# A two-block transformer on one Trainium2 core: how half B of the residual is renewed in the turns of the second block

## The reference, cut to what matters

```
x = x + gt1 * rms_norm(y_lat, g_mix_post[i])
m_lat = sq_relu_mlp(modulate(rms_norm(x, g_mlp_pre[i]), sh2, sc2), w_mlp_in[i], w_mlp_out[i])
x = x + gt2 * rms_norm(m_lat, g_mlp_post[i])
# next layer: modulate(rms_norm(x, g_mix_pre[i + 1]), sh1, sc1), then the projection by w_qkv
```

## Time and profile before

| what | value |
|---|---|
| median of 3 runs | 3484.14 us (3482.54 to 3484.38) |
| the profiled execution, time | 3486.8 us |
| its span in the profile | 3485.0 us |
| PE busy | 3435.7 us (99%), 18494 instructions |
| DVE busy | 2166.1 us (62%), 3570 instructions |
| ACT busy | 1318.3 us (38%), 1951 instructions |
| POOL busy | 297.0 us (9%) |
| mean granted TensorE clock | 0.996 |

### The profile page before, as it was taken

The page is one execution under the profiler, slowest core; times in us unless marked ns, Lnnn a source line. Parts: engine busy times, 40 slices in busy tenths (PEclk is TensorE's granted clock), DMA queues, the critical chain, the costliest instruction groups (busy, mean ns, idle before and its releaser), DMA issues.

```text
span 3485.0 us, 46915 instructions
## 1 busy us (share of the span) xinstructions
PE 3435.7 (99%) x18494; PEld 2869.0 (82%) x18494; DVE 2166.1 (62%) x3570; ACT 1318.3 (38%) x1951; POOL 297.0 (9%) x376
## 2 busy tenths in 40 slices
PE   9999999999999999999999999999999999999998
PEld 7888967898888988895789888899988898588888
DVE  7555565656555655566676777788776557655444
ACT  4222453333222422246333523355523236643222
POOL 0000232001000100023100000012100001210000
PEclk9999999999999999999999999999999999999999
DMA  7544302434444344330243444345444311013221
GB/s 277 187 157 160 109 24 100 157 133 169 155 160 150 137 165 156 146 108 10 102 163 138 148 160 157 145 147 180 173 171 163 112 70 67 25 50 119 89 95 49
DMA packets 85562, 452.01 MB, mean 130 GB/s; under 512 B 10305, under 2 KB 12545, under 8 KB 48609
## 3 DMA queue, kind: packets, MB, share of 16 engines
q1 hardware_dynamic: 83168, 439.10, 34.2%
q0 software_dynamic: 2176, 9.92, 0.8%
HBM read 446.88 MB, written 2.10 MB: 129 GB/s over the span
## 4 chain that ended last, share of the span: by engine, by line
PE 89%; DVE 5%; ACT 3%; issue 1%; DMA 0%; POOL 0%; DVEq 0%; SPq 0%; ACTq 0%; POOLq 0%
PE ps L660 22%; PE ps L658 22%; PE ps L659 22%; PE ps L2774 2%; PE ps L2775 2%; PE ps L2776 2%; PE ps L3473 1%; PE ps L1035 1%; PE ps L1037 1%; ACT P L1855 1%; PE ps L1036 1%; PE ps L1772 1%; PE ps L1295 1%; PE ps L1297 1%; PE ps L1296 1%
## 5 line engine op out<-in xcount | busy, mean ns | idle before, releaser
L660 PE MATMUL ps<-nH,WL 128*128 128x512 f32 x2256 | 884.9, 392 | 0.0
L658 PE MATMUL ps<-nH,WH 128*128 128x512 f32 x2256 | 884.3, 392 | 0.4 <-ACT rot L3203 0.4
L659 PE MATMUL ps<-nL,WH 128*128 128x512 f32 x2256 | 883.1, 391 | 0.0
L564 DVE TENSOR_TENSOR WL<-raw,WH 128x2048 fp32r<-128x2048 f32 (+2 forms) x297 | 651.0, 2196 | 372.3 <-ACT WH L553 371.2
L553 ACT ACTIVATE WH<-raw 128x2048 fp32r<-128x2048 f32 (+2 forms) x299 | 543.3, 1822 | 574.4 <-PE ps L660 496.9
L658 PEld LDWEIGHTS ps<-nH,WH 128*128 128x128 f32 x2256 | 423.8, 188 | 95.2 <-issue 3.3
L659 PEld LDWEIGHTS ps<-nL,WH 128*128 128x128 f32 x2256 | 423.8, 188 | 93.7 <-issue 0.2
L660 PEld LDWEIGHTS ps<-nH,WL 128*128 128x128 f32 x2256 | 423.8, 188 | 91.5
L624 DVE SCALAR_TENSOR_TENSOR araw<-araw,cB 128x1024 f32<-128x1024 f32 x224 | 275.4, 1229 | 208.2 <-DMA araw<-in_ast 207.9
L658 PE MATMUL ps<-hH,WH 128*128 128x512 f32 x944 | 372.2, 394 | 1.0 <-DVE h L1262 1.0
L660 PE MATMUL ps<-hH,WL 128*128 128x512 f32 x944 | 371.3, 393 | 0.0
(11 more groups left out here) (452 smaller groups left out, 5919.6 us busy)
## 6 DMA issues: line engine op xcount, KB each, us to landing
raw<-in_wst SPq DMA_DIRECT2D x273, 1024.0 KB, 4.8
araw<-in_ast SPq DMA_DIRECT2D x225, 512.0 KB, 5.7
raw<-in_wst SPq DMA_DIRECT2D x18, 512.0 KB, 3.3
araw<-in_wst SPq DMA_DIRECT2D x9, 1024.0 KB, 4.8
row<-in_ast SPq DMA_DIRECT2D x15, 512.0 KB, 10.5
cw<-in_cw POOLq DMA_DIRECT2D x4, 1024.0 KB, 6.0
h<-in_xT SPq DMA_DIRECT2D x4, 512.0 KB, 5.5
raw<-in_wst SPq DMA_DIRECT2D x8, 256.0 KB, 2.7
```

The source lines that it names most:

```text
L564: dve.q.tensor_tensor(M.WL[k % NW][:, 0:n], M.raw[raw_use[k]][:, 0:n], M.WH[k % NW][:, 0:n].bitcast(F32), ALU.subtract).then_inc(*v_wlo.up(k))
L658: pe.q.matmul(to, hi[:, i, cc], xh, start=i == 0, stop=False)
L659: pe.q.matmul(to, hi[:, i, cc], xl, start=False, stop=False)
L660: t = pe.q.matmul(to, lo[:, i, cc], xh, start=False, stop=i == nk - 1)
```

## The change

It touches the first and the second turn. The third does what it did before.

1. ACT: half B's tiles of `ma` are multiplied by gain and gate on ACT (`gained(o)`), right behind square o for o = 0 to 5 and ahead of the split of weights in the same step; products 6 and 7 stand behind the root of half B. These are 8 more ACTIVATEs in each of the two turns.
2. DVE: half B is renewed two tiles at a time (`renew_pair`): 4 products and 4 additions of 128x2x256 instead of 8 and 8 of 128x256.
3. DVE: in step i, half A's `times` and `low` come ahead of the renewal.
4. DVE: the first half of the last split comes ahead of the pair of i = 4; the second half comes right behind the pair of i = 6, ahead of the additions of squares 5, 6 and 7, where it stood behind them.
5. ACT's squares of half B's renewed tiles wait for the pair (`i | 1`), and so do later readers of `h` (`was`).

```
             def renewed(x, i):
-                half_square_act(act, g + "AB"[x], lat.half[x], i, hs[x], lambda i: v_h.to(post + "AB"[x], i))
+                half_square_act(act, g + "AB"[x], lat.half[x], i, hs[x], lambda i: v_h.to(post + "AB"[x], i | x))
+
+            def gained(o):
+
+                act.wait_ge(*v_gain.to(post))
+                act.wait_ge(*a_sq.to(post + "B", o))
+                act.q.activation(ma[1](o), ma[1](o), ACT.Copy, scale=der(post)[:, o:o + 1]).then_inc(*a_gt.up(post, o))
...
-                else:
-                    act.wait_ge(*v_gain.to(post))
-                    act.wait_ge(*a_sq.to(post + "B", o))
-                    act.q.activation(ma[1](o), ma[1](o), ACT.Copy, scale=der(post)[:, o:o + 1]).then_inc(*a_gt.up(post, o))
+                if g is None or o < 6:
+                    gained(o)
                 split_act(act, k0 + (6 if o >= 4 else 5 if o == 3 else 4))
...
             half_root_act(act, post + "B", B)
+            gained(6)
+            gained(7)
             for i in range(8):
...
+            def renew_pair(i):
+
+                n = post + "B"
+                u, h = M.ma[:, i:i + 2, B.cols], M.h[:, i:i + 2, B.cols]
+                dve.wait_ge(*mm.to(n, "rstd"))
+                dve.wait_ge(*a_gt.to(post, i + 1))
+                dve.q.tensor_tensor(u, u, B.stat[:, 0:B.N].unsqueeze(1).broadcast_to([128, 2, B.N]), ALU.mult
+                                    ).then_inc(*v_pr.up(n, i))
+                dve.wait_ge(*v_pr.to(n, i))
+                dve.wait_ge(*was(1, i))
+                dve.wait_ge(*was(1, i + 1))
+                dve.q.tensor_tensor(h, h, u, ALU.add).then_inc(*v_h.up(n, i + 1))
...
             half_inverse_dve(dve, post + "B", B)
             for i in range(8):
-                renew(1, i)
                 if i < 4:
                     times(0, i + 4)
                 if i < 5:
                     low(0, i + 3)
-                add(g, 1, i - 1)
                 if i == 4:
                     split_half_dve(dve, k0 + 6, 0)
+                if i % 2 == 0:
+                    renew_pair(i)
+                if i == 6:
+                    split_half_dve(dve, k0 + 6, 1)
+                add(g, 1, i - 1)
             add(g, 1, 7)
-            split_half_dve(dve, k0 + 6, 1)
             half_inverse_dve(dve, g + "B", B)
```

More of the change, by code:

```diff
@@ L2686, in turn_dve @@
                 half_inverse_dve(dve, post + "B", B)
-                n = post + "B"
-                dve.wait_ge(*mm.to(n, "rstd"))
                 for i in range(0, 8, 2):
[L2690 to L2697, removed]
+                    renew_pair(i)
                 return
@@ L3675, in gains @@
                 gain_dve(dve, "latmlp1", V("g_mlp_pre_2", 8), 2, 1, 3)
-            turn_dve(dve, "wopost", "latmlp1", None, lambda x, i: v_h.to("latmlp0post" + "AB"[x], i), der("wopost"), gains,
+            turn_dve(dve, "wopost", "latmlp1", None, lambda x, i: v_h.to("latmlp0post" + "AB"[x], i | x), der("wopost"), gains,
                      k0)
-            drain(mlp2_turn_dve(dve, "latmlp1", None, 1, lambda x, i: v_h.to("wopost" + "AB"[x], i), lambda: None, 3))
+            drain(mlp2_turn_dve(dve, "latmlp1", None, 1, lambda x, i: v_h.to("wopost" + "AB"[x], i | x), lambda: None, 3))
         def rest_pool(pool):
```

## The result

The changed kernel takes 3489.59 us (median of 21 runs, 3486.61 to 3493.17), the kernel before 3484.42 us (median of 21 runs). The ratio is 1.0014 with a 95% interval of 1.0009 to 1.0020, so the change makes the kernel slower by 5.2 us; that is under the 0.2% that the forecast took as the bound, and shows only because of the many runs. The forecast was 3488.7, within a range of 3482.0 to 3491.2. Two single executions of the study, one of e2_early (3765 us) and one of the kernel before (5909 us), fell into a slower state with a mean clock of 0.85 and 0.65 and count in no ratio.

What follows compares the result with a forecast made beforehand. PE, at 89%, was taken as the bound, its waits of 5.6 us capping gains. Turns of +1.35 and +1.95 us (+3.3) plus +1.3 for the clock gave +4.6, 3488.7 us against the median of 3484.14; range 3482.0 to 3491.2.

Steps and rivals of the forecast that it cites:

- Pairs: DVE, half B's renewal: a pair of tiles takes 1.32 us where two renewals took 1.72, gaining 1.6 us a turn.
- `times` and `low` ahead: DVE: one of each fits in the 0.79 us wait for the spread, gaining 0.66 us.
- Products at the head: ACT's products ahead of the split or root delay the head: +0.4 us first turn, +1.0 second.
- ACT's split takes back 1.9 us at low part 7: Loop: DVE stands 1.9 us for ACT's high part 7, leaving 0.4 of the 2.3 us gained.
- From low part 7 to the last addition: DVE's stretch to half B's last addition grows from 6.1 to 7.5 us, +1.45 us a turn.
- Together, +1.45 and +2.05 at the last sum: Delay at half B's sum: first turn 0 + 1.45 us, second 0.6 + 1.45.
- The clock: PE's longer stand at the sum makes the granted clock fall in the first turn too: +1.3 us, likelihood 0.6.
- What the trace would show: Signs: DVE stands 1.9 us before low part 7; PE's sum waits reach 2.6 and 3 us; split-weight wait goes.
- The sum: Both turns: +3.3 us without the clock, plus 1.3 for the clock, +4.6 us in all.
- The cap: PE's waits in both turns, 3.5 + 2.1 = 5.6 us, cap what waits can give.
- The faster rival: ACT's split comes early enough that low part 7 doesn't wait: -0.5 to -3.1 us, 3481.0 us; chance 0.17.
- The slower rival: Longer stand drops the clock in both turns, for two stretches instead of one: +8.1 us, 3492.2 us; chance 0.08.

Runs made afterwards that it cites:

- e2_early: Changed kernel with ACT's split of the last weight block right behind half B's root, ahead of products 6 and 7: +3.2 us against the kernel before.
- e6_nopair: Changed kernel without its pairs and ACT products, half B renewed by the old two instructions: +7.2 us against the kernel before.
- e3_prod: Changed kernel with ACT's products 3, 4 and 5 behind the root of half A: +4.3 us against the kernel before.
- e1_late: Changed kernel with the second half split back behind the last addition: +1.7 us against the kernel before, ratio 1.0005.
- e9_before: The kernel before, unchanged, timed once more as a kernel of its own: +0.7 us against the kernel before.
- e12_order: Kernel before with `times` and `low` ahead of each renewal and ACT's split ahead of the loop, no pairs or products: -0.9 us, ratio 1.0001.
- e7_allfill: e4_all with 8 matmuls of ones ahead of the last sum in both turns: 3480.26 us, 4.5 below the kernel before.
- e4_all: Changed kernel with the edits of e1_late, e2_early and e3_prod together: -1.9 us against the kernel before.
- e11_bsplit: Kernel before with only the second half split moved ahead of the last three additions: +3.7 us against the kernel before, ratio 1.0010.

## Why the prediction was right, and where it wasn't

The forecast was +4.6 us, the measurement +5.2. Point by point:

- **Pairs, 1.32 us, 1.6 gained a turn.** A pair took 1.33. Without pairs and products the turns are 0.7 longer (e6_nopair); the net of both is therefore smaller than the pairs' own gain, as the sum had it; no run has the pairs without the products, so the 1.6 by itself isn't measured.
- **`times` and `low` ahead.** DVE's wait for the spread fell from 0.79 to 0.16 us in the first turn. Right.
- **Products at the head, +0.4 and +1.0.** e3_prod gives 0.41 and 0.73. The second was sized too large: what was late on DVE by 0.94 met 0.2 to 0.3 of slack on PE.
- **ACT's split takes back 1.9 us at low part 7.** DVE stood 1.84 us there, low part 7 came 7.54 us behind the spread (7.4 forecast, 7.82 before), and e2_early takes the wait away: 1.41 and 1.61 of the distance. This was the step that made the forecast slower and not faster, and it held.
- **From low part 7 to the last addition, 6.1 to 7.5 us.** It took 8.0 in the first turn (2872.51 to 2880.50) and 7.65 in the second. This is the term that was sized worst: the last three additions, priced at 1.35 us, took 1.82 and 1.48. The 0.34 between the turns stays open, as said above, and is why e1_late gave more in the first.
- **Together, +1.45 and +2.05 at the last sum.** Measured +2.09 and +2.06. The first was too small by 0.6, of which 0.47 in the stretch behind low part 7. The second is right by luck: the head was 0.27 too large, and the two terms behind it 0.12 and 0.17 too small.
- **The clock, +1.3 in the first turn.** A low stretch of 3.4 us came there. From the first turn's last sum to the second's first the kernel before took 203.53 us (2880.96 to 3084.49; 203.27 in e9_before) and the changed one 204.50 (2880.56 to 3085.06), so the price there was 1.0 to 1.2. Over the profiles this distance is 203.0 to 203.5 in the six without a low stretch, 204.4 to 205.2 in the five with 3.4 us of it and 204.8 to 206.3 in the three with 6.8. In every profile of a kernel that differs from before in these turns and has no filling matmuls it came (8 of 8), in the two of before it did not, and with filling matmuls it never did (4 of 4). But my reason, that the longer stand brings it on, isn't shown: in e12_order PE stands no longer than before, and the clock fell all the same. That the fall hangs on PE's standing still is shown by the filling; why it fell here and not in the kernel before stays open, so this term was right in part by luck.
- **What the trace would show.** I wrote that half A's other low parts would no longer hold PE. The small waits within half A (0.38 and 0.20 us in either turn) did go; the one for the first low part stayed at 1.3 in the first turn, and in the second one of 0.87 is new, with the late head. PE also waited 0.95 and 1.0 us for the last one, which I hadn't forecast: it comes about when it came before while PE gets there sooner. That has no effect on the end, since PE would only have waited at the sum. The wait at the sum was forecast at 2.6 and 3 us and measured at 3.0 and 2.8.
- **The sum.** The turns' 2.09 + 2.06 and the 1.0 behind the first one make 5.1 us, against 5.2 measured. Without the clock I had 3.3, which was 0.85 too small, and the clock's 1.3 was some 0.3 too large; that the total missed by only 0.6 owes something to that. What PE waits behind the sum stayed about even: 0.5 a turn for the split weights went, 0.5 and 0.3 for the spread came, where I had counted on 0.1.
- **The cap.** The gain was capped at PE's waits, 5.6 us. e7_allfill, at -4.5, is under it, with some of that from the clock.

The faster rival needed ACT's split out of the way. e2_early is that condition alone: it gave 1.41 and 1.61 of the 1.9 us a turn that the rival counted on, and both turns were still longer than before, by 0.7 and 0.45. e4_all, which moves the products and the half split as well, comes out 1.9 us below before, where the rival had priced 3.1. The slower rival, two low stretches in a row, did occur in the first turn of three profiles (6.8 us in e1_late, e3_prod and e11_bsplit), though in none of the change itself. Its share of executions can't be read from one profile each, and the 0.9 us by which the first turn started early in the changed kernel's profile, beyond the clock, stays open.

## What to carry to other kernels

Where an engine works in order and another waits for its last result, ask of each instruction not whether it is needed soon but whether it stands ahead of that result: a half split of 1.13 us moved ahead of three additions cost 1.1 to 1.4 us a turn, though it ended a wait of only 0.5 us of its own consumer. A faster engine runs into the next one's queue: shortening DVE by 2.3 us brought half A's last low part only 0.3 us nearer until ACT's 1.9 us split left the way. And a wait on TensorE can cost more than its own length by the clock that falls behind it; a few matmuls of ones in the wait keep it up, and cost 0.3 to 0.4 us a turn here with 7 or 8 of them, since they outlasted the wait; 16 cost up to 0.75.

## What the runs showed of the hardware

Filling PE's wait with matmuls of ones kept the clock up in the two turns in all four kernels that have them; over the whole execution it did not, as those kernels too show low stretches near 10 and 2310 us and behind 3470 us, where PE has little left to do. The kernel before had 3.4 us at the low level in the second turn in both of its profiles; with 7 matmuls of 128x128 ahead of the sum it had none. The length of the stand alone doesn't decide: with waits of 1.1 and 1.0 us the clock fell in the second turn of the kernel before and in the first of e12_order.
The Trainium skill, "TensorE: Matmul & The Clock Gate", section "Part 1: The HAM clock gate (the "warmup" mystery)", says that the monitor runs freely and that where a kernel meets it differs between runs. The traces agree in part: shifting the turns by a few us moved the fall from one turn to the other, but two profiles of the same kernel showed it in the same places, while the stretch near 470 us came and went between kernels whose code up to there is the same.
